# A hybrid mixer and mixture-of-experts layer on one core: the routing step rebuilt, and the loop over heads written out

## What is computed

```
h = concat(meta_tokens (16), x (1024))                 # 1040 rows of 1024
h = h + hybrid_mixer(rms_norm(h, mix_norm_w))          # conv branch and 4 heads of a gated delta rule
xn = rms_norm(h, ffn_norm_w)
group  = argmax_4(xn @ w_group + b_group);  p = its softmax value
logits = (xn @ w_router + b_router)[group]             # 8 experts of that group
e_top  = top-2 of them; w_top = normalized softmax * p
y[token] = sum over its 2 experts: w_top * (silu(xn @ w_gate[e]) * (xn @ w_up[e])) @ w_down[e]
out = rms_norm(h + y, final_norm_w)[16:]
```

## Time and profile before

| | |
|---|---|
| three runs, median (lowest, highest) | 1421.7 us (1421.06, 1423.56) |
| the profiled execution: its own time, its span | 1422.42 us, 1420.6 us |
| TensorE busy, matmul | 1281.9 us, 90% |
| VectorE, ScalarE, GpSimd busy | 64%, 51%, 11% |
| mean granted TensorE clock | 0.955 of full speed |
| HBM traffic over the span | 204 GB/s |

### The profile page before, as it was taken

One profiled execution on the slowest core, in us unless ns is written; L12 is line 12 of the kernel. 1 busy time (PEld: TensorE's weight loads), 2 busy tenths in 40 slices (PEclk: granted clock), 3 DMA queues, 4 the chain that ended last, 5 costly groups with the idle time before them and its releaser, 6 DMA issues. The chain is left out here.

```text
span 1420.6 us, 20123 instructions
## 1 busy us (share of the span) xinstructions
PE 1281.9 (90%) x7438; PEld 1125.2 (79%) x7438; DVE 915.8 (64%) x1141; ACT 719.6 (51%) x920; POOL 160.6 (11%) x143
## 2 busy tenths in 40 slices
PE   6989998999899989989964899999999999999950
PEld 6889997999799989978854788888888888888740
DVE  6753446355545463524236788898888888888818
ACT  7340324123412351523222677777777887777723
POOL 0010111011101120510002111010111111111000
PEclk9999999999999999999985999999999999999985
DMA  7100010011101110318213799999999999999848
GB/s 194 45 16 31 16 35 26 16 30 30 31 16 31 30 30 1 120 54 295 82 60 146 279 362 364 381 379 375 394 371 380 376 382 375 381 376 372 311 161 348
DMA packets 38048, 273.58 MB, mean 193 GB/s; under 512 B 8147, under 2 KB 8403, under 8 KB 25700
## 3 DMA queue, kind: packets, MB, share of 16 engines
q1 hardware_dynamic: 28340, 251.65, 47.5%
q0 software_dynamic: 9216, 16.80, 3.1%
q10 hardware_dynamic: 432, 4.27, 0.8%
HBM read 260.10 MB, written 29.36 MB: 204 GB/s over the span
## 5 line engine op out<-in xcount | busy, mean ns | idle before, releaser
L790 DVE TENSOR_TENSOR w_lo<-w_raw,w_hi 128x2048 fp32r<-128x2048 f32 x192 | 433.7, 2288 | 69.6 <-ACT w_hi L645 69.5
L645 ACT ACTIVATE w_hi<-w_raw 128x2048 fp32r<-128x2048 f32 x192 | 357.2, 1916 | 20.6 <-PE bank L527 12.7
L1136 PE MATMUL bank<-xn_hi,p_hi 128*128 128x364 f32 (+1 forms) x672 | 231.8, 345 | 2.3 <-DVE p_lo L1588 2.3
L1138 PE MATMUL bank<-xn_hi,p_lo 128*128 128x364 f32 (+1 forms) x672 | 219.3, 326 | 0.0
L1137 PE MATMUL bank<-xn_lo,p_hi 128*128 128x364 f32 (+1 forms) x672 | 218.8, 326 | 0.0
L525 PE MATMUL bank<-w_hi,xgT_hi 128*128 128x512 f32 x512 | 207.1, 404 | 2.9 <-DVE xgT_lo L914 2.9
L527 PE MATMUL bank<-w_hi,xgT_lo 128*128 128x512 f32 x512 | 201.8, 394 | 0.0
L526 PE MATMUL bank<-w_lo,xgT_hi 128*128 128x512 f32 x512 | 201.0, 393 | 0.0
L1136 PEld LDWEIGHTS bank<-xn_hi,p_hi 128*128 128x128 f32 x672 | 130.3, 194 | 3.1 <-DVE p_lo L1588 2.7
L1137 PEld LDWEIGHTS bank<-xn_lo,p_hi 128*128 128x128 f32 x672 | 130.3, 194 | 0.4
L1138 PEld LDWEIGHTS bank<-xn_hi,p_lo 128*128 128x128 f32 x672 | 129.4, 193 | 0.0
(11 more groups left out here) (237 smaller groups left out, 2002.2 us busy)
## 6 DMA issues: line engine op xcount, KB each, us to landing
w_raw<-in_w_down SPq DMA_DIRECT2D x32, 2048.0 KB, 10.0
w_raw<-in_w_gate SPq DMA_DIRECT2D x31, 2048.0 KB, 10.6
w_raw<-in_w_up SPq DMA_DIRECT2D x31, 2048.0 KB, 9.6
p_raw<-in_w_tiles SPq DMA_DIRECT2D x28, 512.0 KB, 3.6
arena<-y_rows SPq DMA_DIRECT2D x8, 1024.0 KB, 11.9
arena<-in_tokens SPq DMA_DIRECT2D x10, 416.0 KB
w_out_raw<-in_w_out SPq DMA_DIRECT2D x4, 1024.0 KB, 8.5
arena<-in_tokens SPq DMA_DIRECT2D x8, 512.0 KB, 4.2
```

What stands on the lines that cost most here:

```text
L645: nc.scalar.activation(w_hi[m][:, half], wraw[m][:, half], ACT.Copy).then_inc(hi_done[m], 1)
L790: nc.vector.tensor_tensor(w_lo[m][:, half], wraw[m][:, half], w_hi[m][:, half].bitcast(F32), ALU.subtract).then_inc(lo_done[m], 1)
L1136: nc.tensor.matmul(out[:, 0:n], p_hi[slot][:, k, :], hi, start=(k == 0), stop=False)
L1138: m = nc.tensor.matmul(out[:, 0:n], p_lo[slot][:, k, :], hi, start=False, stop=(k == KD - 1))
```

## The change

1. **Heads.** `for h in range(H)` replaces the hardware loop on four engines. SyncE keeps its loop. TensorE's wait for `sum_act` moves from the end of a head to behind the `grow` round of the next.
2. **Router.** TensorE transposes the rows of h before the norm; `ffn_norm_w` is multiplied into the router weights once (`wr` times `ffc`), and the row's norm factor comes in with the bias in `logits_of`. A row load waits until the tile in its buffer is turned. Turn and router are moved ahead in the order, and the last half tile is copied by VectorE.
3. **Top-2 in two batches.** `choose(0, 5)` runs inside the loop at tile 5, `choose(5, 8)` behind the last tile. Counting is split in the same way.
4. **Tables.** 32 blocks instead of 47. The token table (`tok_vals`, 32 columns) is made first and released by `tables` 1; the table of destinations and weights (`row_vals`, 64 columns) follows and is released by `tables` 2. The copies of `columns` are gone: DMAs and the output scale read the tables.
5. **Overflow.** The lists are built inside the overflow loop, only for a block that is run.
6. **Expert stage.** `hidden(e)` runs between the halves of `split(e, 2)`. The load of the first down unit, and with it that of the second gate unit, waits for `tables` 2 and for the first two gathers; the load of the final norm's weights is moved behind them. ScalarE's output step takes over the wait for the scatter.

```diff
@@ SyncE
                 if t and t + 2 < NT:
                     sp.wait_ge(x2_done, t)
+                    sp.wait_ge(tr_done, 2 * t)
                     load_rows(t + 2)
...
-            sp.wait_ge(tables, 1)
+            sp.wait_ge(tables, 2)
+            sp.wait_ge(gathered[0], 16)
+            sp.wait_ge(gathered[1], 16)
             load_unit(sp, 0, 2)
-            sp.dma_start(fw, fin_w).then_inc(fw_loaded, 16)
...
             refill(1, 0, 1)
+            sp.dma_start(fw, fin_w).then_inc(fw_loaded, 16)
@@ TensorE, output product and router
-            def turn_rows(t):
-                pe.wait_ge(x2_done, t + 1)
+            def turn_half(t, b):
+                pe.wait_ge(res_done, 2 * t + b + 1)
...
+                    last = t == NT - 1 and b == 1
+                    out_product(t, b, range(5 if last else KD))
...
+                    if t >= 5 and b == 1:
+                        router(t - 1)
+                    if last:
+                        turn_half(t, 0)
+                        out_product(t, b, range(5, KD))
+            turn_half(NT - 1, 1)
+            router(NT - 1)
@@ TensorE, tables
             for n in range(2 * NT):
                 if n % NT == 0:
-                    pe.wait_ge(r_dve, TABLE_END if n else TABLE_IN)
-                m = nc.tensor.matmul(bank[2][:, 0:2 * BLOCKS], slot1h[:, n, :], vals[:, n].rearrange("p a b -> p (a b)"),
+                    pe.wait_ge(r_dve, SLOT_B if n else SLOT_A)
+                m = nc.tensor.matmul(bank[0][:, 0:E], slot1h[:, n, :], tok_vals[:, n, :], start=(n == 0),
+                                     stop=(n == 2 * NT - 1))
+            m.then_inc(r_pe, 1)
+            pe.wait_ge(r_dve, ROW_VALS)
+            for n in range(2 * NT):
+                m = nc.tensor.matmul(bank[1][:, 0:2 * E], slot1h[:, n, :], row_vals[:, n].rearrange("p a b -> p (a b)"),
                                      start=(n == 0), stop=(n == 2 * NT - 1))
@@ VectorE
+            for t in range(3, NT - 1):
                 residual(t)
...
+                if t == 5:
+                    dve.wait_ge(lg_done, SEEN)
...
+                    n = choose(0, SEEN)
                 normed(t)
...
+            n = choose(SEEN, NT)
...
             dve.wait_ge(r_pe, 3)
+            ts(itab[:, 0:E], bank[0][:, 0:E], float(BIG), None, ALU.add).then_inc(tables, 1)
+            step(tt(row_vals[:, :, 0, :], hot1, per(const("dst"), E), ALU.mult), wait=False)
+            n = step(tt(row_vals[:, :, 1, :], hot1, per(weight, E), ALU.mult), wait=False)
             split(0, 0)
...
+            dve.wait_ge(r_pe, 4)
+            ts(stab[:, 0:E], bank[1][:, 0:E], float(BIG), None, ALU.add)
+            nc.vector.tensor_copy(wtab[:, 0:E], bank[1][:, E:2 * E]).then_inc(tables, 1)
@@ VectorE, one expert
                 turned(e + 1, 1 - p)
-                if before is not None:
-                    dve.wait_ge(scattered[p], before * 16)
-                columns(e + 3, 1 - p, e, p)
-                split(e, 2)
+                split(e, 2, [0])
                 hidden(e, p)
+                split(e, 2, [1])
@@ GpSimd
-            pool.wait_ge(icol, 1)
-            gather(0)
-            gather(1)
+            pool.wait_ge(tables, 1)
+            gather(0, 0)
+            gather(1, 1)
@@ TensorE, heads (ScalarE, VectorE and GpSimd alike)
                 rnd(h, "grow")
+                if h:
+                    pe.wait_ge(sum_act, sums(h - 1, "o"))
...
-                    pe.wait_ge(sum_act, sums(h, "o"))
...
-            with pe.Fori(0, H - 1) as h:
-                mixer(h, False)
-            mixer(H - 1, True)
+            for h in range(H):
+                mixer(h, h == H - 1)
```

More of the change, by code:

```diff
@@ L184, in layer_kernel @@
         small = keep.take(4, 40)
+        ffs = [small[:, 0, 3 * t:3 * t + 3] for t in range(NT)]
         stat = keep.take(2, 4)
@@ L497, in tail_tensor @@
-            nc.tensor.matmul(bank[0][:, 0:NT * E], strict, flat, start=True, stop=False)
-            for t in range(NT - 1):
-                n = NT - 1 - t
-                m = nc.tensor.matmul(bank[0][:, (t + 1) * E:NT * E], ones, ecnt[:, t, :].unsqueeze(1).to_broadcast([128, n, E]),
-                                     start=False, stop=(t == NT - 2))
+                        if b == 1:
+                            router(0)
+                    if t == 4:
+                        turn_rows(2 + b)
+                        router(1 + b)
@@ new lines, in tail_tensor @@
+            for t in range(SEEN):
+                nc.tensor.matmul(bank[3][:, 0:E], ones, ecnt[:, t, :], start=(t == 0), stop=False)
+            pe.wait_ge(r_dve, COUNT_B)
+            nc.tensor.matmul(bank[2][:, SEEN * E:NT * E], strict, late, start=False, stop=False)
+            for t in range(SEEN, NT - 1):
+                m = nc.tensor.matmul(bank[2][:, (t + 1) * E:NT * E], ones,
+                                     ecnt[:, t, :].unsqueeze(1).to_broadcast([128, NT - 1 - t, E]), start=False,
+                                     stop=(t == NT - 2))
@@ L502, in tail_tensor @@
+            m.then_inc(r_pe, 1)
+            for t in range(SEEN, NT):
+                m = nc.tensor.matmul(bank[3][:, 0:E], ones, ecnt[:, t, :], start=False, stop=(t == NT - 1))
             m.then_inc(r_pe, 1)
@@ L580, in over @@
             def over(j):
+                pe.wait_ge(r_dve, j * OVER_STEPS + (ROUTED + OVER_LIST))
+                for n in range(2 * NT):
+                    m = nc.tensor.matmul(bank[5][:, 0:4], oho[:, n, :], oval[:, n, :], start=(n == 0), stop=(n == 2 * NT - 1))
+                m.then_inc(r_pe, 1)
                 turn(j + E, 0, j * 16 + 16 * (E // 2 + 1))
@@ L908, in tail_vector @@
-            nc.vector.tensor_copy(over_i[0:1, :], ofl[0:1, :]).then_inc(over_done, 1)
-            split(0, 0)
+                n = step(tt(slot1h[:, v], row(iota[:, 0:128], NT), per(rank[:, v], 128), ALU.is_equal), wait=False)
+                assert n == (SLOT_B if half else SLOT_A), (n, "SLOT")
+            dve.wait_ge(r_act, 2)
+            wk = weight.rearrange("p (t k) -> p t k", k=2)
+            step(red(tk[2], grp_v[1], ALU.add), wait=False)
+            step(ts(tk[5], tk[4], 1.0, None, ALU.add))
@@ L932, in tail_vector, with expert @@
             turned(1, 1)
-            columns(3, 1, 0, 0)
             split(0, 2)
             hidden(0, 0)
-            def expert(e, p, before):
+            def expert(e, p):
                 split(e, 1, [0])
@@ L1572, in mixer @@
                 norm(h, "o", 1.0 / 128, ob)
-            with act.Fori(0, H - 1) as h:
-                mixer(h, False)
-            mixer(H - 1, True)
+            for h in range(H):
+                mixer(h, h == H - 1)
             tail_scalar(act)
```

402 lines of the change are left out of this document (207 added, 195 removed).

## The result

The changed kernel takes 1398.92 us in the median of four runs (1397.42 to 1401.63), the kernel before 1421.38 (four runs, 1420.83 to 1423.56). The ratio is 0.984, with a 95% interval of 0.983 to 0.985: 22.5 us less, where 30.2 were forecast. The profiled execution took 1397.42 us with a span of 1395.4, TensorE's mean granted clock 0.966. It is 1.5 us faster than the median of its kernel and the profiled one of the kernel before 1.0 us slower than its own, so the two spans differ by more than the medians do, by 25.2 us.

The account below looks back on a forecast made before the run. The prediction took TensorE to set the pace nearly everywhere, standing still in three places. 9.85 + 12.3 + 8.0 = 30.2 off 1422.42 gave 1392.2, with 0.7 to the median 1391.5 us; range 1380 to 1403, the forecast's own 1384 to 1399.

Parts of the forecast that it names:

- part 1: Heads without a loop: two looped boundaries become like the straight third; 9.85 us less, bounds 0 and 9.85 + 7.
- part 3: Expert period: the wait for `hidden` before `hid_turn`, 0.36 us in 28 periods, goes; 8.0 us less, bounds 0 and 10.1.
- part 2: Routing: expert 0 starts 15.3 us earlier, less 3 for late loads; 12.3 us less, bounds 7 and 19.
- DMA sets the period: Rival for the expert period: DMA, busy for 99%, sets it, so part 3 gives nothing; 1399.5 us, chance 0.15.
- the term taken from the third boundary: `ktr` to `mtr` at both looped boundaries falls from 26.02 and 26.17 to 21.17; 4.85 + 5.00 us.
- the bounds 0 and 9.85: Gain in the heads: 0 if written-out code stalls elsewhere, the whole 9.85 us if sequential code streams in.
- The moved wait: TensorE's wait for `sum_act` in the heads: worth 0.77 us at the third boundary, counted as nothing.
- the rival that hoped for `p_lo` going first: Full clock and free port: tables at full clock (6 us), `p_lo` first at head boundaries (up to 7); about 1381, chance 0.15.
- The late gate unit: Routing into expert 0: second gate unit lands at about 775, ScalarE wants it at 771.8; about 3 us lost.
- The rest of TensorE's period has no gap: Expert period: with `hidden` 2.2 us earlier, no other wait remains on TensorE; at most 10.1 us gained.
- Part 4: Overflow and end: 15 skipped passes are hidden by VectorE's 20.57 us idle before its first sum; they cost nothing.
- the slower rival: Overflow loop is the new end: skipped passes stall 4.19 us each, 42 more; 1433.8 us, chance 0.03.

Follow-up runs that it names:

- e7_less_dma: e3_order with only half of each gate unit loaded from expert 2 on, every instruction kept, output no longer the layer's; ratio 0.9745.
- e1_loops: The kernel before with only its head loops written out on four engines, the wait for `sum_act` left in place; 1418.65 us, ratio 0.9972.
- e2_moved: e1_loops with TensorE's wait for `sum_act` moved behind `grow` of the next head; 1416.02 us, ratio 0.9954.
- e4_hidden: The changed kernel with `hidden(e)` put back behind both halves of `split(e, 2)` in VectorE's queue; 1406.93 us, ratio 0.9888.
- e12_scatter: e4_hidden with the scatter wait moved from ScalarE's `y_out` to VectorE ahead of `split(e, 2)`; 1406.28 us, ratio 0.9888.
- e3_order: The changed kernel with GpSimd's multiplication `qg` waiting for VectorE's `p_lo` of the same head; 1385.16 us, ratio 0.975.
- e6_both: e3_order with VectorE making `hidT_lo` ahead of both halves of `split(e, 1)` and ScalarE `hidT_hi` between its halves; 1377.01 us, ratio 0.9702.
- e8_gate_first: e3_order with the second gate unit's load ahead of the first down unit's in SyncE's queue; 1386.16 us, ratio 0.9753.
- e9_late_gather: e3_order with GpSimd's gathers waiting for both tables instead of the token table alone; 1393.81 us, ratio 0.9798.

## Why the prediction was right in its range and 7 us off

1391.5 was forecast and 1398.92 measured, inside 1380 to 1403 and just inside the forecast's own 1384 to 1399. Against the spans, part 1 gave 3.1 us less than forecast and part 3 5.6 less, while part 2 gave 2.9 more and the end 0.9; that these halve the miss, to 5 us, was luck. The other 2.4 us lie between profile and medians: 0.7 was allowed for the kernel before, and the median of the changed one is 1.5 above its profiled execution. The number is that of the rival "DMA sets the period" (1399.5), but e7_less_dma refutes the mechanism: the time went elsewhere.

**Part 1: 9.85 forecast, 6.71 measured; the first step that failed.** That code written out has no stand at `grow` is right. The failing step is the term taken from the third boundary, with "What follows `mtr` in heads 0 to 2 repeats to within 0.1 us, so this is a pure shift". Of the 3.3 us that heads 1 and 2 lack, 1.0 is ahead of `mtr` (21.53 and 21.82 instead of 21.17) and 2.3 behind it (121.73 and 121.62 from `mtr` to the next `ktr` instead of 120.54). That boundary of the kernel before is one that ran without a clock dip. In the five kernels with written-out heads and the blocked `p_lo` (changed, e1_loops, e2_moved, e4_hidden, e12_scatter), 13 of 15 boundaries have it. The looped heads had a dip behind `mtr` too, only the later of the two, so a head without either gives 6.4 us (146.56 to 140.19) and one with both gives 3.3. Between the bounds 0 and 9.85 the trace is on the side of what the Trainium skill (Runtime: NRT & Kernel Launch, Instruction fetch mechanics) says of sequential code: from 90 to 625 us no engine of the changed kernel stands for more than 0.5 us without a releaser, where TensorE of the kernel before has 4.19 and 4.26. The moved wait was rightly counted at nothing, and the rival that hoped for `p_lo` going first priced it too low, at 2.3 us a boundary and 7 in all: it is 2.7 to 3.4 us up to `mtr`, and 13.0 in all with the dips behind `mtr` that go with it. TensorE coming earlier doesn't bring it: GpSimd's multiplication starts at 231.35, 0.07 us after ScalarE's L1571 ends, as the forecast said. It takes an order between the two, e3_order.

The Trainium skill (SBUF — State Buffer, Who interferes with whom) says that a VectorE instruction with two SBUF inputs contends with a GpSimd instruction that reads SBUF, and one with at most one SBUF input doesn't. The traces agree: `p_lo` (both inputs in SBUF) took 3.93 beside the multiplication and 1.22 ahead of it, while L1772, with one input in PSUM, took 1.36 either way.

**Part 2: 12.3 forecast, 15.2 measured.** The chain was right nearly step by step. From the last output product: logits 3.9 forecast and 3.74 measured, `choose(5, 8)` 5.2 and 5.0, ranks and first half of `slot1h` 4.4 and 4.4, token table 7.2 and 7.2, gather 1.2 and 1.1 behind it. The first gather's descriptors took 1.38 us where 2.8 was forecast. To the turn it came to 28.9 instead of 29.8: a little less at several steps, and nothing for the gather, whose rows were there before the second table was done. The output product lost 2.80 (2.9 forecast). The tables ran at half clock, so that rival falls. The late gate unit, at 3 us, was right in kind and somewhat high: it landed 12.6 us after its issue, ScalarE waited 2.05 for it, and TensorE's stand in front of the second gate product grew from 1.35 to 3.52. What the forecast lacked is what this stand hides: the one for `hidden` ahead of the first `hid_turn` shrank from 2.71 to 0.93 us, and the fall of the clock moved ahead of it, so that the stretch lost only 1.23 and the first period gained 1.96.

**Part 3: 8.0 forecast, 2.39 measured, the largest miss; only 0.43 of it is the repeating period.** The other 1.96 are the first period's, as above. The wait before `hid_turn` did go, and with it 0.41 us a period. "The rest of TensorE's period has no gap" held only while that wait was there: `hidT_lo` is made behind a half of the next up unit's split, and with TensorE earlier it comes 0.12 to 0.38 us late. e6_both removes that and gets the period of 17.73 (17.8 was forecast), 9.7 us. Moving `hidden` is itself worth 4.34 us there, e4_hidden shows; some 2 us net (566.71 against 564.76 with `hidden` in its old place) are lost to something in the new expert stage that stays open.

**Part 4: nothing forecast; 0.04 measured at the end.** The skipped overflow passes cost nothing, so the slower rival falls. The stretch from the last `hid_turn` to the first final sum is 0.84 us shorter, which I had not counted, and its cause stays open. `hidden`'s place does not explain it: e12_scatter, with `hidden` put back, has 22.23, and e8_gate_first and e9_late_gather, with it early, 22.81 and 22.90. In part it goes with the clock: over the first 10 us of the stretch it was 0.83 in the changed kernel, e3_order and e12_scatter, but 0.69 in the kernel before, 0.66 in e4_hidden and 0.70 in e8_gate_first and e9_late_gather.

## What to carry to other kernels

Before you price a wait that goes, list what else is ready just behind it: here each of two waits was replaced at once by the next one in VectorE's queue, and one reordering each (GpSimd behind `p_lo`, `hidT` ahead of a split half on both engines) gave 13.0 and 9.7 us, together nearly as much as the large change. Before you credit an edit with a stretch, look at where a fall of the clock lies in it, since it can move to the next stretch and make a gain of one column and a loss of the other. Before you take a row of a favourable stretch as the price of several, look at the granted clock in that row and in its like, since one boundary without a dip is a sample of one. An engine at 99% is a suspect, not a bound, until a run with less of its work has been timed.

## What the runs showed of the hardware

- The granted clock of TensorE fell to its lower level behind a stand of 2.5 to 3.4 us ahead of `mtr` in 13 of 15 boundaries and not in the other two, where the stand was 3.2, with the same instructions; both dips of a head together cost 3.1 us. Behind a stand of 0.5 us at the same place it fell in none of 24, though the later dip still came in some heads.
- `p_lo` was held for as long as GpSimd's multiplication ran, and a little longer: 1.22 us became 3.93.
- A gather's or scatter's descriptors on GpSimd are held by VectorE too. They took 0.97 to 1.20 us with no `w_lo` split beside them. In all 105 cases in the 14 traces where they began while a half of VectorE's split (both inputs in SBUF) ran, they ended 0.86 to 0.89 us after the end of a half: in 101 the same half, in 4 the one behind it. That is the difference between the 1.70 us of the changed kernel (the half that ran ended at 747.08, the gather at 747.95) and the 4.66 of the kernel before, which stood through both halves of `split(0, 0)` (over at 771.60, the gather at 772.49). The DMA engines moved 399 GB/s under the 4.66 and 84 under the 1.70, but the loads alone do it neither: at 754.00 in the changed kernel, with 309 GB/s from 752 to 760 and no split beside it, a gather took 0.98. So the forecast was right to trust the 4.66 more than what it quotes of the Trainium skill there. Why a few gathers stand through a second half is open.
